# Filler products on TensorE in the waits for the norms ahead of three feed-forward blocks

## The reference

```
def rms_norm(x, g):
    y = x * rsqrt(mean(x * x, axis=-1) + eps)
    return y * g

h = h + rms_norm(mixer(rms_norm(h, g0)), g1)
h = h + rms_norm(ffn(rms_norm(h, g2)), g3)
```

## Time and profile before

| | |
|---|---|
| median of three runs | 3585.28 us (3585.12 to 3588.91) |
| the profiled execution | 3584.79 us, of which its span is 3583.0 us |
| mean granted clock of TensorE | 0.981 |
| TensorE matmul (PE) busy | 3460.6 us, 97% of the span |
| VectorE (DVE) busy | 2307.8 us, 64% |
| ScalarE (ACT) busy | 1787.2 us, 50% |
| GpSimd (POOL) busy | 487.4 us, 14% |
| HBM | 174 GB/s over the span |

### The profile page before, as it was taken

The page is one execution under the profiler, slowest core; times in us unless marked ns, Lnnn a source line. Parts: engine busy times, 40 slices in busy tenths (PEclk is TensorE's granted clock), DMA queues, the critical chain, the costliest instruction groups (busy, mean ns, idle before and its releaser), DMA issues.

```text
span 3583.0 us, 62262 instructions
## 1 busy us (share of the span) xinstructions
PE 3460.6 (97%) x21616; PEld 3015.8 (84%) x21616; DVE 2307.8 (64%) x3462; ACT 1787.2 (50%) x2734; POOL 487.4 (14%) x538
## 2 busy tenths in 40 slices
PE   9997999999999999999999999999799999999998
PEld 7885888888888888887888888887688788888887
DVE  5687565555555766675666677778755665565566
ACT  4477454545454554544555444454344554454453
POOL 0001400011114100124100001105011000000005
PEclk9998999999999999999999999999899999999999
DMA  6561545555555555443455555666235455556555
GB/s 210 171 187 54 185 145 193 184 193 182 193 184 192 168 189 174 161 150 129 148 189 197 188 188 195 203 222 218 58 112 188 141 189 193 183 188 193 184 188 187
DMA packets 190641, 626.67 MB, mean 175 GB/s; under 512 B 26822, under 2 KB 40200, under 8 KB 190360
## 3 DMA queue, kind: packets, MB, share of 16 engines
q1 hardware_dynamic: 179948, 612.49, 52.3%
q10 hardware_dynamic: 10572, 12.56, 1.2%
HBM read 620.52 MB, written 3.15 MB: 174 GB/s over the span
## 4 chain that ended last, share of the span: by engine, by line
PE 89%; DVE 7%; ACT 2%; issue 1%; DMA 1%; POOL 0%; ACTq 0%; DVEq 0%; SPq 0%; POOLq 0%
PE bank L1895 53%; PE bank L1898 28%; PE m L1918 2%; DVE w_lo L1038 1%; PE m L1920 1%; PE m L1908 1%; DVE prod L1708 1%; DVE w_lo L1042 0%; DVE y L1065 0%; ACT w_hi L462 0%; DMA w_raw<-stream 0%; PE m L2429 0%; DVE st L1711 0%; PE bank L2372 0%; DVE st L1713 0%
## 5 line engine op out<-in xcount | busy, mean ns | idle before, releaser
L1038 DVE TENSOR_TENSOR w_lo<-w_raw,w_hi 128x1024 fp32r<-128x1024 f32 x1086 | 1335.2, 1251 | 778.6 <-ACT w_hi L462 773.1
L1895 PE MATMUL bank<-act,w_hi 128*128 128x512 f32 x6016 | 1512.8, 393 | 8.6 <-DVE w_lo L1038 7.9
L462 ACT ACTIVATE w_hi<-w_raw 128x1024 fp32r<-128x1024 f32 x1090 | 1128.9, 1054 | 405.8 <-PE bank L1898 357.4
L1895 PEld LDWEIGHTS bank<-act,w_hi 128*128 128x128 f32 x6016 | 1082.8, 189 | 209.1 <-DVE w_lo L1038 8.9
L1898 PEld LDWEIGHTS bank<-act,w_lo 128*128 128x128 f32 x6016 | 822.3, 191 | 59.0
L1898 PE MATMUL bank<-act,w_lo 128*128 128x256 f32 x6016 | 840.2, 283 | 0.0
L1895 PE MATMUL bank<-ffn,w_hi 128*128 128x512 f32 x2432 | 613.6, 393 | 2.4 <-DVE w_lo L1042 2.2
L471 ACT ACTIVATE low<-bank 128x256 f32<-128x256 f32 x542 | 207.6, 383 | 761.4 <-PE bank L1898 760.3
L1895 PEld LDWEIGHTS bank<-ffn,w_hi 128*128 128x128 f32 x2432 | 436.2, 189 | 81.6 <-DVE w_lo L1042 3.4
L1046 DVE TENSOR_TENSOR ev<-bank,low 128x256 f32<-128x256 f32 x468 | 198.2, 423 | 243.8 <-ACT low L471 239.0
L1898 PEld LDWEIGHTS bank<-ffn,w_lo 128*128 128x128 f32 x2432 | 333.9, 190 | 25.2
(11 more groups left out here) (414 smaller groups left out, 2245.3 us busy)
## 6 DMA issues: line engine op xcount, KB each, us to landing
w_raw<-stream SPq DMA_DIRECT2D x1148, 512.0 KB, 3.4
b_part<-s_bt ACTq DMA_DIRECT2D x16, 256.0 KB
pow_b<-powers ACTq DMA_DIRECT2D x16, 256.0 KB
bias<-toeplitz SPq DMA_DIRECT2D x4, 512.0 KB, 9.1
out<-res SPq DMA_DIRECT2D x3, 512.0 KB, 2.8
res<-x_t SPq DMA_DIRECT2D x2, 512.0 KB, 8.8
res<-x_t ACTq DMA_DIRECT2D x2, 512.0 KB, 10.8
bias<-toeplitz SPq DMA_DIRECT2D x4, 256.0 KB, 11.2
```

The lines of the kernel that those rows point to most:

```text
L462: a(w_hi[:, q, :], w_raw[:, q, :], ACT.Copy).then_inc(hi_ready, 1)
L1038: e.tensor_tensor(w_lo[:, q, :], w_raw[:, q, :], w_hi[:, q, :].bitcast(F32), ALU.subtract).then_inc(lo_ready, 1)
L1895: mm(bank[w][:, 0:2 * n], w_hi[:, q, wt], x(h * hk + k, 0, 2 * n), start=(h == 0 and k == 0), stop=False)
```

## The change

A helper issues products of `ones` with the identity (float32, 128x128x128) into bank `m[3]`, whose content nobody reads at that point. At each of the three places four of them go behind the products of line 1981, four behind those of line 1984, and twelve behind the product of line 1994. The numbers of every wait stay as they were. The other norms (`post_mlp`, `post_ffn0`, `post_ffn1`) are not touched.

```
+        def keep_busy(n):
+            for _ in range(n):
+                mm(m[3][:, 0:P], ones[:, :], ident[:, :], start=True, stop=True)
+
-        def norm(name, squares=None, kt=DT):
+        def norm(name, squares=None, kt=DT, fill=0):
             if squares is None:
                 pe.wait_ge(y_squares, YSQ[name] + 2 * (DT - 1) + 1)
                 for tb in range(2):
                     mm(m[5][:, tb:tb + 1], ssum[:, 128 * tb:128 * tb + 128], ones[:, 0:1], start=(tb == 0), stop=False)
+                keep_busy(fill)
                 pe.wait_ge(last_square, POSTS.index(name) + 1)
                 for tb in range(2):
                     last = mm(m[5][:, tb:tb + 1], sq[:, 2, 128 * tb:128 * tb + 128], ones[:, 0:1], start=False, stop=(tb == 1))
                 last.then_inc(sum_spread, 1)
+                keep_busy(fill)
                 return
...
-        def spread(name):
+        def spread(name, fill=0):
             pe.wait_ge(rstd_ready, NORM[name] + 1)
             mm(bank[0][:, 0:T], ones[:, :], rms[:, :], start=True, stop=True).then_inc(sem("rstd_spread"), 1)
+            keep_busy(fill)
...
-            norm("post1")
-            spread("post1")
+            norm("post1", fill=4)
+            spread("post1", fill=12)
...
-            norm("post2")
-            spread("post2")
+            norm("post2", fill=4)
+            spread("post2", fill=12)
...
-            norm("post_s5")
-            spread("post_s5")
+            norm("post_s5", fill=4)
+            spread("post_s5", fill=12)
```

## The result

The changed kernel takes 3576.41 us (median of 10 executions, 3572.75 to 3578.73) against 3585.24 us for the kernel before (10 executions, 3583.70 to 3588.91): ratio 0.9974, 95% interval 0.9966 to 0.9982. It is 8.8 us faster, about 0.25%. I had forecast 3584.9 us in a range of 3580.0 to 3589.5 us, and had given 0.04 to a gain of this size. A repeat gave 3574.67 us against 3585.10 us, ratio 0.9972 (0.9961 to 0.9983).

What follows compares the result with a forecast made beforehand. TensorE's own work was taken to bound the kernel, busy for 97% of the span. Shifts of -0.25 us at `post1`, -0.25 at `post2` and +0.1 at `post_s5` made -0.4 us on the median: 3584.9 us, range 3580.0 to 3589.5 us.

Steps and rivals of the forecast that it cites:

- What bounds it: Whole kernel: TensorE, busy for 97% of the span and 89% of the chain; only moving its own work moves the end.
- the prize: First pairs at `post1`, `post2`, `post_s5` and the latter's spreading product: full clock would win at most 5.05 us.
- What the fill costs: In TensorE's waits at the three places: nothing at full clock at `post1`; twelve products at half clock take 5.4 us.
- The step that failed: At `post1`, behind the stretch from 444.3 us: the clock falls at 447.7 us despite the fill.
- my doubt: At the three places: fill products of 128 columns, 0.11 us apart per instruction, may not hold the clock as dense products do.
- The likeliest case's sum: All three places, clock falls all the same: -0.25 - 0.25 + 0.1 = -0.4 us, 3584.9 us; chance 0.50.
- my upper bounds there: Tile 3 of the first pair, clock back as late as before: +0.4 us at `post1` and `post2`, +1.3 us at `post_s5`.
- My -0.9 us: `post1`, same at `post2`: clock back one stretch earlier, at 451.1 us, so tile 3 starts at 454.1 us.
- Rival (a): Clock holds at all three places: -5.05 us, 3580.2 us, down to 3578.5 us if the fall at 481.8 us goes; chance 0.27.
- the fall behind the 2 us wait: Behind `post1`, at 481.8 us: half clock for 3.4 us, costing 1.7 us, may go if the clock holds.
- Rival (b): Clock falls before the twelve start, fill overruns into tile 0: 2.2 us at each place, 6.6 us, 3591.9 us; chance 0.10.
- Rival (c): At the three places the clock behaves as before and the fill ends before tile 0: 3585.3 us; chance 0.13.

Runs made afterwards that it cites:

- the second wait filled too: Changed kernel plus 8, 6 and 6 products between the halves of the second pair's second unit, against the kernel before: 3576.67 us, ratio 0.9974.
- one place: Fill at `post1` alone, 20 of the 60 products, none at `post2` and `post_s5`, against the kernel before: 3580.87 us, ratio 0.9988.

## Why the prediction was wrong

**What bounds it, and the prize: right.** I had worked out 1.47, 1.53 and 0.52 + 1.53 us for a clock that holds, 5.05 us in all. The three places measure 1.6, 1.5 and 1.7 us in the mean of four, and 2.2 us at `post_s5` between the first two profiles (28.86 - 26.64).

**What the fill costs: right.** 24 records take 2.84 us and end 0.56 us ahead of tile 0; a product costs 0.22 us; at half clock the 24 take 5.17 us, by my sum 5.4 us.

**The step that failed: "I take it that the clock falls at 447.7 us as before".** It didn't, in any of the four profiles at `post1` and `post2`, nor in three of four at `post_s5`. I had measured the fill against one stretch, 1628.7 to 1632.1 us, because it ended in products of the same kind. But that stretch also holds 3.40 - 2.21 = 1.19 us in which TensorE stood idle. In the changed kernel the stretch from 442.4 to 445.8 us has 0.07 us of idle time by the records. I looked at which kind of product a stretch ended in and not at how much of it was filled: by my own numbers the stretch before 447.7 us would hold 1.30 us of old records and eight products of 0.22 us, 3.1 of 3.40 us, more than any of the three rows that I compared it with, and I called it "nothing dense". That the idle time is what let the clock fall at 1632.1 us is argued from these rows; no run shows it. The one-column run shows that my doubt wasn't empty: densely recorded but unstreamed products let the clock fall and then overrun, just as I had described. With the 128 columns of the change it held, but for one profile at `post_s5`, and with 64, in one profile, at two places of three. The Trainium skill's rule that activity of the array releases the throttle (TensorE: Matmul & The Clock Gate, Part 1: The HAM clock gate), which I had set against the row at 1628.7 us, gave the right side at `post1` and `post2` in all four profiles of the changed kernel.

**The likeliest case's sum (-0.4 us)** fell with that step. Its overrun is real where the clock does fall: in the run with one column 0.4 us at `post1` and 1.3 us at `post_s5`, the same as my upper bounds there, but 2.1 us at `post2`, where my bound was 0.4 us. My -0.9 us for a clock that comes back one stretch earlier takes the tiles to run faster than the 1.13 us that I had given them; at 1.13 us it is -0.6 us.

**Rival (a), the clock holds,** is the case that came. Its time of 3580.2 us was still 3.8 us too high. I had named the fall behind the 2 us wait as one that may go with it, worth 1.7 us; it went in two of four executions (1.55 us each, 0.8 us in the mean). I hadn't summed the falls of the mixers: the state-space stage gives 1.8 us, the stages ahead of `post1` and between the first block and `post2` 1.3 us.

**Rival (b), the overrun,** is what 24 products do, at full clock. **Rival (c)** is excluded by the stage table.

**The range** ended at (a)'s own time and left nothing below it for the shifts that I had written down beside the sum (1.7 us for each fall elsewhere). With two of them it would have reached to 3576.8 us, still 0.4 us above the result.

**What stays open.** 8.8 us in the medians (10.4 us in the repeat) against 4.9 us at the places. The rest lies in stages that were not changed. That it goes with where the clock's falls lie in them is my reading of their low stretches; no run shows it by itself. In the state-space stage, executions of all kernels, with fill and without, take from 316.9 to 322.4 us, and most of that spread lies in one part of it, between 42 and 67 us behind `post_ffn0`. With four profiles of each kernel I can't say whether the changed one meets the better positions there as a rule, as a consequence of ending its earlier stages sooner, or by chance; the gap in the medians of ten against ten and of seven against twenty-five executions suggests that it does so as a rule. Other kernels point the same way: the medians gain 7.9 us against 3.5 us at the places with only the long wait filled, 8.4 against 5.7 us with the second wait filled too (its own 1.5 us counted), 6.2 against 3.1 us with 64 columns. With 24 products it is 0.7 against 0.7 us. What the fill causes directly is shown only for the 4.9 us.

## What to carry to other kernels

Where an engine on the chain waits a few microseconds at a time for other engines, read the granted clock in the stretch behind the wait, and price the half-speed products there: that is what idle work in the wait was shown to win (4.9 us here; the other 4 us of the median are not traced to it). Here the filler had to stream (one column kept nothing), had to fill the short waits ahead of the long one as well where one of them was long enough to lose the clock alone (2.2 us at `post_s5`), and had to end ahead of the real work at full clock: twelve products of 0.22 us won and twenty-four lost it again. Judge such a change by the stages that it touches in several profiles, since the medians also hold falls of the clock elsewhere that come and go: single stages that the change doesn't touch differed by up to 6.6 us between profiles.

## What the runs showed of the hardware

- The records of products with a 128x128 float32 weight load (two to a product) start 0.11 us apart at full clock and 0.21 us apart at half clock, whether they stream 1, 64 or 128 columns (24 one-column records, about the first seven at full clock and the rest at half, took 4.40 us; 24 of 128 columns, nearly all at half clock, took 5.17 us). The clock did answer to the columns: with one column it fell at all three places (one profile), with 128 at one place in one of four profiles.
- The same wait of 2.0 us let the clock fall in some executions (18.2 us for the stage) and not in others (16.65 us), with the same instructions around it. The Trainium skill says that the moment of the change varies from run to run (TensorE: Matmul & The Clock Gate, Part 1: The HAM clock gate); the traces agree, and here it decides whether there is a fall at all, at 1.55 us each.
- The 64x64 products of the state-space stage answer to the clock as well. The first 128 behind the taps took 5.20 us with 2.8 us of them at half clock (only the long wait filled), 5.69 us with 3.9 us (kernel before) and 6.65 us with 6.0 us (one place): about 0.45 us more for each microsecond at half clock, by my estimate from these three.
